# A hybrid RWKV-7 / convolution / MoBA / RetNet trunk: the LoRA products as one fp32r pass over 96 stacked rows

## The reference

```python
p = p + (token_shift(p) - p) * mu
r, k, v, wl, al = jnp.split(p, [G, 2*G, 3*G, 3*G + L], axis=-1)      # G = 256, L = 32
decay = jnp.exp(-RWKV_DECAY_SCALE * jax.nn.sigmoid(w0 + jnp.tanh(wl) @ w2))
a = jax.nn.sigmoid(a0 + al @ a2)
kk = normalised per head (k * k_k);  k = k * (1 + (a - 1) * k_a)
...
bonus = jnp.sum(rh * kh * r_k, axis=-1, keepdims=True) * vh
```

## Time and profile before

| | |
|---|---|
| time, median of 3 runs | 576.5 us (576.31 to 576.83) |
| time of the profiled execution | 576.78 us |
| its span, from the first to the last instruction | 575.0 us |
| TensorE busy | 567.4 us, 99% of the span |
| VectorE, ScalarE, GpSimd busy | 66%, 48%, 43% |
| mean granted TensorE clock | 0.997 |

### The profile page before, as it was taken

How to read it: one execution, slowest core, us unless ns; L and a number is a source line. 1 busy time by engine, 2 the same in 40 slices (tenths; PEclk the granted TensorE clock), 3 DMA queues, 4 the chain that set the end, 5 groups by cost and what they waited for, 6 DMA issues and landing times. The chain is left out here.

```text
span 575.0 us, 12739 instructions
## 1 busy us (share of the span) xinstructions
PE 567.4 (99%) x5244; PEld 464.0 (81%) x5244; DVE 381.0 (66%) x644; ACT 278.3 (48%) x555; POOL 249.3 (43%) x197
## 2 busy tenths in 40 slices
PE   9999999999999999999999999999999999999995
PEld 7978888888877777888898788888888777788884
DVE  4999976482488557774543897947537865778163
ACT  5486231343574475534656743324357335735253
POOL 4946552044941323536335455402386313145340
PEclk9999999999999999999999999999999999999998
DMA  9546634056432122353535423332743321224513
GB/s 281 161 130 206 212 97 111 8 130 149 109 79 75 39 75 62 113 171 132 165 117 139 111 77 108 88 70 58 161 127 83 77 73 39 73 75 147 184 40 143
DMA packets 103373, 64.58 MB, mean 112 GB/s; under 512 B 29151, under 2 KB 94227, under 8 KB 103316
## 3 DMA queue, kind: packets, MB, share of 16 engines
q1 hardware_dynamic: 103316, 63.77, 39.4%
HBM read 55.61 MB, written 8.14 MB: 111 GB/s over the span
## 5 line engine op out<-in xcount | busy, mean ns | idle before, releaser
L706 POOL TENSOR_TENSOR w_lo<-w_raw,w_hi 128x512 fp32r<-128x512 f32 x156 | 216.6, 1409 | 283.0 <-ACT w_hi L1295 277.7
L772 PE MATMUL bank<-act_hi,w_hi 128*128 128x512 f32 x432 | 173.2, 401 | 0.0
L775 PE MATMUL bank<-act_lo,w_hi 128*128 128x512 f32 x432 | 168.5, 390 | 0.0
L774 PE MATMUL bank<-act_hi,w_lo 128*128 128x512 f32 x416 | 162.3, 390 | 0.0
L1295 ACT ACTIVATE w_hi<-w_raw 128x512 fp32r<-128x512 f32 x140 | 80.3, 622 | 74.1 <-PE bank L857 28.2
L772 PEld LDWEIGHTS bank<-act_hi,w_hi 128*128 128x128 f32 x432 | 81.1, 188 | 24.7 <-issue 8.2
L775 PEld LDWEIGHTS bank<-act_lo,w_hi 128*128 128x128 f32 x432 | 81.1, 188 | 17.4
L774 PEld LDWEIGHTS bank<-act_hi,w_lo 128*128 128x128 f32 x416 | 78.2, 188 | 14.8
L1221 PE MATMUL bank<-w_hi,act_hi 128*128 128x512 f32 x128 | 50.0, 390 | 0.0
L1223 PE MATMUL bank<-w_hi,act_lo 128*128 128x512 f32 x128 | 49.8, 389 | 0.0
L1222 PE MATMUL bank<-w_lo,act_hi 128*128 128x512 f32 x128 | 49.8, 389 | 0.0
(11 more groups left out here) (217 smaller groups left out, 961.0 us busy)
## 6 DMA issues: line engine op xcount, KB each, us to landing
w_raw<-in_w_in_dram SPq DMA_DIRECT2D x62, 512.0 KB, 4.1
w_raw<-in_w_out_dram SPq DMA_DIRECT2D x16, 512.0 KB, 3.8
pages<-in_x_dram SPq DMA_DIRECT2D x4, 512.0 KB, 6.3
x_or_y<-in_x_dram SPq DMA_DIRECT2D x4, 512.0 KB, 4.2
x_scratch<-x_or_y SPq DMA_DIRECT2D x4, 512.0 KB, 2.9
x_or_y<-x_scratch SPq DMA_DIRECT2D x4, 512.0 KB, 3.7
out_dram<-pages SPq DMA_DIRECT2D x8, 256.0 KB, 2.2
bias_scratch<-pages SPq DMA_DIRECT2D x1, 1280.0 KB, 8.1
```

The costliest lines, as they stand in the source:

```text
L706: ins = pool.tensor_tensor(low, raw, w_hi[:, i % HI, k, 0:n].bitcast(F32), ALU.subtract)
L772: mm(b[:, :], hi, act_hi[:, k, :], start=n == 0, stop=False)
L774: mm(b[:, :], lo, act_hi[:, k, :], start=False, stop=False)
L775: ins = mm(b[:, :], hi, act_lo[:, k, :], start=False, stop=n == KT - 1)
```

## The change

- The LoRA weights are no longer four blocks of 32 rows by 128 columns, loaded as they are. Both matrices are loaded three times, at the partitions 0, 32 and 64 (six DMAs in place of four, each row twice as long), into a page that is free so early. GpSimd turns them into fp32r: two multiplications by one over 96 rows before the low part of tile 6, and two subtractions over 32 rows before that of tile 7, so that the three blocks of rows hold high, low and high parts.
- ScalarE's `lora_tanh` is one tanh on 32 rows and four copies of 32 rows (`stat_hi`, rows 0 to 63); a new step `lora_low` on VectorE, in front of `kk_unit 1`, makes rows 64 to 95, the low parts, with two subtractions.
- TensorE's `lora` is four fp32r matmuls over 96 rows, and is issued behind v0's product in place of in front of it.
- The step `bonus` moves from in front of `rotate rq0` to in front of `scores 0`, behind the product of rk0.
- At the start VectorE awaits each half of the norm's weights where it uses it first, and TensorE's seven idle products after the norm's weights become one.
- ScalarE's v0 waits for GpSimd's four LoRA operations in layer 0, since the raw weights lie in the page of v.

```diff
-  ..., ("lora_tanh",), ("shift", "r1"), ("kk_unit", 1), ("lora",), ("shift", "v0"), ("decay_scan",), ...
+  ..., ("lora_tanh",), ("shift", "r1"), ("lora_low",), ("kk_unit", 1), ("shift", "v0"), ("lora",), ("decay_scan",), ...
-    s += [("copy", "rq0"), ("copy", "rq1"), ("bonus",), ("rotate", "rq0"),
-          ("copy", "rk0"), ("rotate", "rq1"), ("scores", 0), ...
+    s += [("copy", "rq0"), ("copy", "rq1"), ("rotate", "rq0"),
+          ("copy", "rk0"), ("rotate", "rq1"), ("bonus",), ("scores", 0), ...
-        lora_w = sb("lora_w", [4 * LORA, DEPTH, P])
+        lora_w = sb("lora_w", [3 * LORA, 2, DEPTH, G], F32R)
+        lora_raw = page(2)[0:3 * LORA].rearrange("p (z l c) -> p z l c", z=2, l=DEPTH)
# SyncE
-            for p in range(2):
-                for r, w in ((2 * p, rwkv_w2), (2 * p + 1, rwkv_a2)):
-                    load(lora_w[r * LORA:(r + 1) * LORA], w[:, :, p * P:(p + 1) * P].rearrange("l k c -> k l c"), "const_b")
+            for r in range(3):
+                for z, w in enumerate((rwkv_w2, rwkv_a2)):
+                    load(lora_raw[r * LORA:(r + 1) * LORA, z], w.rearrange("l k c -> k l c"), "lora_loaded")
# GpSimd, at the head of tile i
+                if i == 6:
+                    pool.wait_ge(s("lora_loaded"), 16 * 6)
+                    for z in range(2):
+                        pool.tensor_tensor(lora_w[:, z], lora_raw[:, z], one[0:3 * LORA].unsqueeze(2).to_broadcast([3 * LORA, DEPTH, G]), ALU.mult).then_inc(s("lora_weight"), 1)
+                if i == 7:
+                    pool.wait_ge(s("lora_weight"), 2)
+                    pool.wait_ge(s("w_split"), i)
+                    low = slice(LORA, 2 * LORA)
+                    for z in range(2):
+                        pool.tensor_tensor(lora_w[low, z], lora_raw[low, z], lora_w[low, z].bitcast(F32), ALU.subtract).then_inc(s("lora_weight"), 1)
+                    pool.wait_ge(s("lora_weight"), 4)
# TensorE, start
-            idle(3)
             pe.wait_ge(s("const_a"), 16)
             turn(0, 0)
             turn(1, 0)
-            idle(4)
+            idle(1)
# TensorE, lora
-                    pe.wait_ge(*at("lora_in", layer))
-                    for p in range(2):
-                        for z, r0 in (("zw", 2 * p * LORA), ("za", (2 * p + 1) * LORA)):
-                            b = begin(f"{z}{p}", layer)
-                            end(mm(b[:, :], lora_w[r0:r0 + LORA, layer, :], WA[r0:r0 + LORA, :], start=True, stop=True, tile_position=(r0, 0)), f"{z}{p}", layer)
+                    if layer == 0:
+                        pe.wait_ge(s("lora_weight"), 4)
+                    for p in range(2):
+                        for z, name in enumerate(("zw", "za")):
+                            pe.wait_ge(*at("lora_in", layer, 2 - z))
+                            b = begin(f"{name}{p}", layer)
+                            end(mm(b[:, :], lora_w[:, z, layer, p * P:(p + 1) * P], stat_hi[0:3 * LORA, z, :], start=True, stop=True), f"{name}{p}", layer)
# ScalarE, v0 and lora_tanh
+                        if job == "v0" and layer == 0:
+                            act.wait_ge(s("lora_weight"), 4)
-                    go(WA[2 * LORA:4 * LORA], WA[0:2 * LORA], ACT.Copy).then_inc(s("lora_copied"), 1)
-                    act.wait_ge(*at("lora_copied", layer))
-                    for r0 in (0, 2 * LORA):
-                        go(WA[r0:r0 + LORA], WA[r0:r0 + LORA], ACT.Tanh).then_inc(s("lora_in"), 1)
+                    go(WA[0:LORA], WA[0:LORA], ACT.Tanh).then_inc(s("lora_bent"), 1)
+                    for z in (1, 0):
+                        if z == 0:
+                            act.wait_ge(*at("lora_bent", layer))
+                        for r in range(2):
+                            go(stat_hi[r * LORA:(r + 1) * LORA, z, :], WA[z * LORA:(z + 1) * LORA], ACT.Copy).then_inc(s("lora_high"), 1)
                     weight_high("r0", layer)
# VectorE, start
-            for a in range(2):
-                dve.wait_ge(*full(f"nw{a}", -1))
             for two in (0, 2):
                 for t in (two, two + 1):
                     invert_root(t, 0)
                     for a in range(2):
+                        if t == 0:
+                            dve.wait_ge(*full(f"nw{a}", -1))
# VectorE, new step
+                def lora_low():
+                    for z in (1, 0):
+                        dve.wait_ge(*at("lora_high", layer, 4 - 2 * z))
+                        r = slice(z * LORA, (z + 1) * LORA)
+                        tt(stat_hi[2 * LORA:3 * LORA, z, :], WA[r], stat_hi[r, z, :].bitcast(F32), ALU.subtract).then_inc(s("lora_in"), 1)
```

More of the change, by code:

```diff
@@ L145, in layer_steps @@
     s += [("shift", "k0"), ("shift", "k1"), ("kk_input",), ("shift", "wa"), ("shift", "r0"), ("kk_square",),
-          ("kk_norm",), ("kk_unit", 0), ("lora_tanh",), ("shift", "r1"), ("kk_unit", 1), ("lora",), ("shift", "v0"), ("decay_scan",), ("shift", "v1"),
+          ("kk_norm",), ("kk_unit", 0), ("lora_tanh",), ("shift", "r1"), ("lora_low",), ("kk_unit", 1), ("shift", "v0"), ("lora",), ("decay_scan",), ("shift", "v1"),
           ("decay_exp",), ("factors", 0), ("gate", "rwkv", 0), ("factors", 1), ("gate", "rwkv", 1), ("factors", 2)]
-    s += [("copy", "rq0"), ("copy", "rq1"), ("bonus",), ("rotate", "rq0"),
-          ("copy", "rk0"), ("rotate", "rq1"), ("scores", 0), ("scores", 1), ("copy", "rk1"), ("rotate", "rk0"), ("to_rows", "v"), ("scores", 2),
+    s += [("copy", "rq0"), ("copy", "rq1"), ("rotate", "rq0"),
+          ("copy", "rk0"), ("rotate", "rq1"), ("bonus",), ("scores", 0), ("scores", 1), ("copy", "rk1"), ("rotate", "rk0"), ("to_rows", "v"), ("scores", 2),
           ("scores", 3), ("wide", 0, 0), ("wide", 0, 1), ("rotate", "rk1"), ("wide", 0, 2), ("wide", 0, 3),
@@ L453, in trunk_kernel @@
             "sq_first": NT, "sq_base": 1, "sq_last": NT, "h_weighted": NT,
-            "kk_sq": 2, "kk_unit": 2, "lora_in": 2, "lora_copied": 1, "decay_sum": 2,
+            "kk_sq": 2, "kk_unit": 2, "lora_in": 2, "lora_high": 4, "lora_bent": 1, "decay_sum": 2,
             "decay_exp": 4, "beta": 1, "kappa": 1, "alpha": 3, "rho": 3, "rkv": 2, "pads": 1, "blocks_done": 1, "blocks_turned": 1, "ret_prefix": 1, "ret_inner": 1, "conv_tap": 2, "ln_scaled": 2, "ln_affine": 2,
@@ L889, in kk_square @@
                     if layer == 0:
-                        pe.wait_ge(s("const_b"), 16 * 6)
+                        pe.wait_ge(s("const_b"), 16 * 2)
                         pe.wait_ge(s("mean_r"), 1)
@@ L1427, in inverse_eye @@
                     else:
-                        act.wait_ge(s("const_b"), 16 * 6)
+                        act.wait_ge(s("const_b"), 16 * 2)
                     go(Xe.rearrange("p s j c -> p (s j) c"), const("eye64").unsqueeze(1).to_broadcast([P, 4 * HEADS, CH]), ACT.Copy)\
@@ L1673, in _ @@
             dve.wait_ge(s("derived"), 5)
-            dve.wait_ge(s("const_b"), 16 * 6)
+            dve.wait_ge(s("const_b"), 16 * 2)
             link(dve.tensor_copy(lmask[:, :], mask_words))
@@ L2065, in _ @@
                 run = dict(shift=shift, kk_input=kk_input, ret_low=lambda: stat_low("ret", RSQ),
-                           ln_square=lambda: stat_low("ln", LNS), kk_unit=kk_unit, decay_scan=decay_scan, factors=factors, bonus=bonus,
+                           ln_square=lambda: stat_low("ln", LNS), kk_unit=kk_unit, lora_low=lora_low, decay_scan=decay_scan, factors=factors, bonus=bonus,
                            gate=gate, scores=scores, block_rows=block_rows, inverse_x=inverse_x, corner_x=corner_x, rotate=rotate,
```

## The result

The changed kernel took 583.25 us (median of four runs, 582.46 to 584.69) against 576.58 (576.31 to 576.83); the ratio is 1.0119 (95% interval 1.0095 to 1.0143). The forecast was 580.0, its range ended at 581.3. The direction was right, the size was not. The profiled execution took 582.51 us, with a span of 580.7.

What follows compares the result with a forecast made beforehand. TensorE, busy 99% of the span, was taken as the bound. Span 575.0 + 4.0 (layer 0) - 0.2 (layer 1) = 578.8, plus 1.8 around it 580.6; median 580.3, stated as 580.0; own range 577.7 to 581.4, 8-in-10 range 576.5 to 581.3.

Steps and rivals of the forecast that it cites:

- Then 0.92 and v1's 5.44: rwkv_g0 starts at 58.1: Layer 0, TensorE after waiting for lora_low until 51.7: LoRA products, then v1; rwkv_g0 4.0 us later than 54.02.
- the clock, as a rival with 0.05: Start: with six idle products gone, k0's matmuls run at low clock, up to 1 us on top, 581; chance 0.05.
- The start, -0.5: Before tile 5: norm and transposes start earlier, and TensorE reaches kk0 at 34.99 instead of 35.49.
- The multiplications, +2.1 on L1690: Layer 0 before kk0: GpSimd's two multiplications hold VectorE's port, L1690 1.3 to 2.1 us later, kk0 at 36.95.
- The subtractions, +1.7: Layer 0 before the first reciprocal: GpSimd's subtractions hold VectorE 1.25 to 2.5 us, 1.7 taken; reciprocal ends at 47.3.
- lora_low's end, 51.7: Layer 0: VectorE's two low-part subtractions, taken as held by GpSimd, end at 51.7, bounds 49.3 to 52.2.
- The pass: LoRA products on TensorE: four fp32r matmuls take 0.92 us instead of 1.27, saving 0.35 us a layer.
- Layer 1, -0.2: Layer 1: TensorE gains 0.35 us, less 0.15 for small waits; bounds -0.35 and +0.6.
- ScalarE's two more operations: lora_tanh: five ScalarE operations for three, 1.0 us more; in layer 0 tile 7's high part starts at 44.7.
- the savings stand: Rival: GpSimd's four operations fall into VectorE's waits and lora_low is in time; 575.3 us, chance 0.10.
- only the first wait comes: Rival: multiplications hold L1690 but lora_low is in time; rwkv_g0 1.1 us later, layer 1 -0.35, 577.2 us; chance 0.13.
- 96 rows cost as much as four row tiles: Rival at the LoRA products: no gain from the new form, 0.7 us less saved, inside the range; no chance given.

Runs made afterwards that it cites:

- start_only: The kernel before with only the start's two edits: one idle product for seven, norm's weights awaited by halves; 576.08 us, ratio 0.9992.
- fill_wide: The changed kernel with three idle products of 512 columns before layer 0's LoRA products; 581.61 us, ratio 1.0085.
- no_port: The changed kernel without GpSimd's four LoRA operations: one ScalarE copy makes the weights' high part, their low part's product is left out; 578.5 us, ratio 1.0038.
- late_lora: The kernel before with one edit: the old LoRA products one tile later, behind v0's; 576.45 us, ratio 0.9996.
- subs_only: The changed kernel with one ScalarE copy in place of GpSimd's two multiplications, its two subtractions kept; 581.83 us, ratio 1.0085.
- port_only: The kernel before plus six raw LoRA weight loads and GpSimd's four operations, their result unused; 578.94 us, ratio 1.0045.

## Why the prediction missed

**The step that failed** is "Then 0.92 and v1's 5.44: rwkv_g0 starts at 58.1". It counts 28 steps of 0.227 us behind a wait of 3.0. The wait came (3.2), and behind it the clock was at its lower level: 8.05 us for 6.36, 1.7 us that the sum did not have; with idle products in the wait 1.6 of them came back. I did weigh the clock, as a rival with 0.05, but at the start, where idle products were removed, and not behind the long wait that my own sum had just put there. At the start it cost little: in the change k0's matmuls start 0.12 us apart from the second on, as before, in start_only from the fifth on, and start_only was no slower.

The clock also seems to widen the runs: with idle products in the wait they lie closer together. The four of the change had a mean clock of 0.993 to 0.995 (before 0.997 to 0.999 over a span) and spans from 580.7 to 582.9, so the median lies 0.7 us above the profiled execution, which was one of the two fastest. I had put it 0.3 below. With 1.9 us of span and the 0.3 that I took off at the end, because the port's terms looked more likely too large, this is the whole miss of 3.25 us: 1.9, 1.0 and 0.3.

**The rest of the sum, term by term.**
- The start, -0.5: the transposes started at 7.58 (7.55 worked out), TensorE was ready for kk0 at 34.86 (34.99). Right.
- The multiplications, +2.1 on L1690: 1.6. The order of the turns was another (copies held, not L1709), the port time much the same. kk0 at 36.55 for 36.95.
- The subtractions, +1.7: the first reciprocal ended at 46.91 for 47.3; against the earlier trace rows and less the 1.6 that is 1.8, in the copies (4.04 us for 2.91) and the maximum (1.04 for 0.41), as worked out. Right.
- lora_low's end, 51.7: 51.71. Right to the digit with some luck, as the first subtraction took 0.98 and the second 1.64.
- Its bounds, 49.3 to 52.2, held; without GpSimd's operations it ended at 48.4. The range printed for the time, 577.7 to 581.4, doesn't quite follow from the bounds of the two layers, which give 577.9 to 581.6 for the median, and the chances named for "slower" add up to 0.81, not 0.79; the measured time lies outside either range.
- The pass: four steps of 0.92. They take 1.00 to 1.04 behind a wait (1.04 in fill_wide, 1.00 in no_port), so some 0.25 is saved, not 0.35; this 0.1 is in the 1.7 above.
- Layer 1, -0.2: +0.56. lora_low's two subtractions were both held by GpSimd (3.02 us), so the LoRA waited 0.27 and the pass saved nothing there; then the second rq waited 0.2 for VectorE to read the gate's bank, and other small waits. I had looked for room only at VectorE's read of v0 (329.33); it is the gate's read, which the second rq waits for, that has none. Mis-sized by 0.76, just inside its bound of +0.6.

```profile
328.78 3.02 DVE L1743 TENSOR_TENSOR stat_hi<-pages,stat_hi 32x512 fp32r<-32x512 f32 x2
```
```profile
331.35 0.39 PE L786 MATMUL bank<-act_lo,w_hi 128*128 128x512 f32 x1
331.85 1.19 PE L914 MATMUL bank<-stat_hi,lora_w 96*128 96x512 f32 x4
```

- Not in the sum at all: a gap without a cause in the profile that the kernel before had near 131 us and the changed one has not. It and some hundredths around it are worth -0.6.
- ScalarE's two more operations, "+1.0": I followed them to tile 7's high part and GpSimd's low part, not to SP's next load, ScalarE's later queue, the scan and the gate. In the change as it is this lies under the LoRA's wait; with that wait shortened it is worth 1.5 us.

In sum: 578.8 + 1.7 (clock) + 0.1 (LoRA's start) + 0.8 (layer 1) - 0.6 (gap) = 580.8, measured 580.7.

**Costed at nothing.** The bonus: right. The two more DMAs and ScalarE's wait for `lora_weight`: nothing hung on them in any trace. The later place of the LoRA, which had no term of its own: the place itself cost nothing (late_lora).

**The rivals.** That the savings stand needed room for the multiplications, which was not there. That only the first wait comes: both came. The clock: it came, but at the LoRA and not at the start. That 96 rows cost as much as four row tiles: they don't, 1.00 to 1.04 us stand against 1.27, but layer 1 shows that a short wait for VectorE's two new subtractions takes the gain back.

## What to carry to other kernels

When a sum puts an idle wait of some 3 us on a TensorE that was never idle, price the clock behind it: here 1.7 us on top of 3.2, and three idle products in the wait brought 1.6 back. Preparing a weight once by four GpSimd operations looks free where GpSimd is idle, but here they cost 4.7 us, about a third of it through the clock, because VectorE was using that gap and was itself just in time for TensorE. And an operation added to ScalarE's queue is to be followed to the loads behind the buffer it frees late.

## What the hardware showed that I had not expected

- After waits of 3.2 us TensorE's granted clock went to 0.5 in both kernels that had such a wait unfilled, for 3.4 and 6.8 us; after waits of 0.9 (no_port) and 1.5 (kk0) it did not, nor with idle products in the wait. The Trainium skill, "TensorE: Matmul & The Clock Gate", section "HAM oscillation — how this bites in real kernels", says that a TensorE that waits too long between bursts starts the next one at the lower clock; the traces agree. The fall was recorded at 51.87 in the change, when the burst had just begun, and at 48.80 in subs_only, 2.0 us into the wait.
- Small bias copies on VectorE, one input and 4 to 20 elements a row, wait a whole GpSimd operation like the large ones (one copy took 1.01 us, where undisturbed ones start 0.07 us apart). The Trainium skill, "SBUF — State Buffer", section "Who interferes with whom", counts copies among the operations that can contend; the trace agrees.
- Two kernels with 24 more matmuls in the LoRA's wait had a gap of 1.9 to 2.2 us at TensorE's 839th matmul with no semaphore behind it. The one with 6 more had none there, but one of 0.38 us behind 964 matmuls. The kernel before has one of 0.46 us behind 966, and so has port_only, which runs the same TensorE program; late_lora, with as many matmuls ahead of that place in a slightly different order, has none. The gaps follow or lie in runs of more than a hundred small matmuls of 64 columns. Two pairs of traces show them at the same place, and late_lora shows that the count alone doesn't settle it; what happens there is open.
- In the first 12 us the view by windows gives a clock of 1.00 while the 128-column steps are 0.213 us apart, twice those later (0.111): the clock record starts only at 10.8 to 13.4 us, about when the steps shorten, so at the start the steps are to be read, not the column.
